# Routing steps of tokens 0 to 127: six per pair of gathers for pairs 0 to 16 and four for pairs 17 to 32, in place of six, five and four

## The reference, cut to what matters

```python
s = jnp.einsum('bshpd,hpkd->bshpk', q, sub_keys)
v_half, i_half = lax.top_k(s, PEER_TOPK)
cand = v_half[..., 0, :, None] + v_half[..., 1, None, :]
top_s, top_c = lax.top_k(cand.reshape(B, S, PEER_HEADS, PEER_TOPK * PEER_TOPK), PEER_TOPK)
experts = i1 * PEER_NKEYS + i2
g = jax.nn.softmax(top_s.astype(jnp.float32), axis=-1)
...
u = expert_u[ec]
act = jax.nn.gelu(jnp.einsum('cd,ced->ce', xc, u).astype(jnp.float32))
return jnp.einsum('ce,ced->cd', gc * act, expert_v[ec])
```

## Time and profile before

| | |
|---|---|
| median of 3 runs | 1257.31 us (1254.69 to 1258.04) |
| the profiled execution, its own time | 1260.68 us |
| its span | 1258.9 us |
| mean granted TensorE clock | 0.944 |
| busy: PE, DVE, ACT, POOL | 1078.0, 796.0, 456.8, 295.8 us |
| moved by DMA | 432.08 MB, mean 343 GB/s |

### The profile page before, as it was taken

One profiled execution on the slowest core, in us unless ns is written; L12 is line 12 of the kernel. 1 busy time (PEld: TensorE's weight loads), 2 busy tenths in 40 slices (PEclk: granted clock), 3 DMA queues, 4 the chain that ended last, 5 costly groups with the idle time before them and its releaser, 6 DMA issues.

```text
span 1258.9 us, 13841 instructions
## 1 busy us (share of the span) xinstructions
PE 1078.0 (86%) x5002; PEld 536.8 (43%) x5002; DVE 796.0 (63%) x1865; ACT 456.8 (36%) x1257; POOL 295.8 (23%) x261
## 2 busy tenths in 40 slices
PE   6998986977887676769988789968998998999998
PEld 2887572432343222313332344423443444565543
DVE  5567758887763999764457667576655477645201
ACT  1132127555342444443353343434334423332201
POOL 0000013434343344433323333332323000000000
PEclk9999987998898889989999899988999999999999
DMA  9987419999999999999999999999999975344573
GB/s 388 409 328 316 169 47 370 364 354 411 421 383 421 417 404 395 378 423 401 421 421 420 421 421 420 420 422 363 421 420 423 380 268 200 142 160 154 212 293 127
DMA packets 63487, 432.08 MB, mean 343 GB/s; under 512 B 6931, under 2 KB 10300, under 8 KB 11836
## 3 DMA queue, kind: packets, MB, share of 16 engines
q0 software_dynamic: 36864, 268.45, 52.4%
q1 hardware_dynamic: 26160, 161.76, 32.3%
q10 hardware_dynamic: 396, 0.99, 0.2%
HBM read 430.12 MB, written 1.06 MB: 343 GB/s over the span
## 4 chain that ended last, share of the span: by engine, by line
PE 51%; DVE 20%; DMA 19%; ACT 5%; issue 2%; POOL 1%; another core or an unknown queue 0%; SPq 0%; DVEq 0%
PE ps L1140 22%; DMA AR<-in_puv,idx 17%; PE ps L1095 10%; DVE AR L1722 7%; PE ps L771 4%; PE ps L1254 3%; PE ps L990 2%; DMA W<-in_w_mod 2%; PE ps L1121 1%; PE ps L806 1%; POOL AR L2513 1%; PE ps L1035 1%; ACT av L2258 1%; DVE RT L1694 1%; ACT acc L2137 1%
## 5 line engine op out<-in xcount | busy, mean ns | idle before, releaser
L2513 POOL DMA_INDIRECT AR<-in_puv,idx x256 | 295.5, 1154 | 675.4 <-PE ps L1095 433.1
L1095 PE MATMUL ps<-AR,acc 128*64 128x512 f32 x904 | 286.6, 672 | 100.2 <-ACT acc L2137 98.4
L1722 DVE CUSTOM_DVE_ANT_0 AR<-AR,mixT 128x1024 f32<-128x1024 f32 x128 | 153.5, 1222 | 69.6 <-DMA AR<-in_puv,idx 69.3
L1140 PE MATMUL ps<-W,AR 128*128 128x512 f32 x416 | 189.2, 598 | 0.7 <-ACT AR L2137 0.7
L1095 PEld LDWEIGHTS ps<-AR,acc 128*64 128x64 f32 x904 | 71.8, 146 | 263.8 <-ACT acc L2137 169.5
L1722 DVE CUSTOM_DVE_ANT_0 AR<-AR,tok 128x1024 f32<-128x1024 f32 x128 | 153.0, 1220 | 48.4 <-DMA AR<-in_puv,idx 48.3
L1140 PE MATMUL ps<-W,hT 128*128 128x512 f32 x320 | 158.4, 626 | 6.5 <-DVE PT L2029 5.2
L2256 ACT ACTIVATE av<-av 128x1 f32<-128x1 f32 x256 | 51.3, 200 | 286.7 <-DVE av L1722 286.1
L1140 PEld LDWEIGHTS ps<-W,AR 128*128 128x128 f32 x416 | 76.1, 191 | 78.8 <-issue 76.7
L1140 PEld LDWEIGHTS ps<-W,hT 128*128 128x128 f32 x320 | 58.1, 198 | 83.3 <-issue 74.7
L2137 ACT ACTIVATE acc<-fold,av 128x64 f32<-128x64 f32 x226 | 78.6, 348 | 7.4
(11 more groups left out here) (459 smaller groups left out, 1311.2 us busy)
## 6 DMA issues: line engine op xcount, KB each, us to landing
W<-in_w_in SPq DMA_DIRECT2D x90, 1024.0 KB, 11.5
W<-in_w_mod SPq DMA_DIRECT2D x24, 1024.0 KB, 16.0
W<-in_wba SPq DMA_DIRECT2D x8, 1024.0 KB
W<-in_wbb SPq DMA_DIRECT2D x8, 1024.0 KB
W<-in_wo SPq DMA_DIRECT2D x8, 1024.0 KB
W<-in_w_out SPq DMA_DIRECT2D x4, 1024.0 KB, 5.7
W<-in_wq SPq DMA_DIRECT2D x4, 1024.0 KB
AR<-in_puv,idx POOLq DMA_INDIRECT x256
```

The lines of the kernel that those rows point to most:

```text
L1095: t = mm(of(("E", a, c))[64 * g:64 * g + 64, :], dg_at((2 * p + g) % NDG, late), GB[:, places[g], D + c * 512:D + c * 512 + 512], start=(m ...
L1140: t = mm(b[:, :], src[:, k, :], slab(i)[:, k, :], start=(k == 0), stop=(k == 7))
L1722: ttr(GB[:, n, 0:D], GB[:, n, 0:D], H2[a][g], 1.0, 0.0, MUL, ADD, av[:, a, c:c + 1]).then_inc(*ve.sig("dot", p, g))
L2513: eng.indirect_dma_start(GB[:, n, :], None, puv, bass.IndirectOffsetOnAxis(ap=idx[:, a, c:c + 1], axis=0)).then_inc(*gp.dma(f"g{n}", "gat" ...
```

## The change

One line of `loop_chores`:

```diff
@@ -492,7 +492,7 @@
-        advance(routes, 6 if p < 8 else 5 if p < 16 else 4 if p < 33 else 8)
+        advance(routes, 6 if p < 17 else 4 if p < 33 else 8)
```

## The result

The changed kernel takes 1252.64 us (median of 13 runs, 1249.65 to 1256.56), the kernel before 1257.31 us on the same chip (13 runs). The ratio is 0.9969 with a 95% interval of 0.9957 to 0.998, 3.9 us less; on a second chip it was 0.996 (0.9945 to 0.9975), 5.0 us less. Forecast were 1250.5 us and 6.8 less.

The account below looks back on a forecast made before the run. Transferred bytes at about 421 GB/s were taken to bound the kernel from 183 to about 976 us, then PE. Terms of 2.0 and 4.8 us took 1257.3 to 1250.5 us; range 1246.5 to 1258, own range 1248.5 to 1253.

Parts of the forecast that it names:

- likeliest case: Both terms count: 1250.5 us, own range 1248.5 to 1253, chance 0.43.
- Hole 1: 268 to 281 us at 272 GB/s, 4.6 us missing; pair 16 was to be issued 4.0 us earlier, pair 17 2.0.
- The chain to the accumulation of pair 25: Pairs 15 to 25, through four attn_mm: its end was to come 2.0 us earlier.
- the hole at 348: 348 to 368 us at 359 GB/s, 2.9 us missing; said to be opened by lateness of pair 25's accumulation.
- term 1: Lead of the chain ending in pair 25's accumulation, 2.0 us; bounds 0 and 4.0.
- Term 2: 460 to 530 us: second routing one pair earlier removes most of DVE's lag, 4.8 us; bounds 0 and 6.2.
- hole 3: 460 to 530 us at 384 GB/s, 6.2 us missing; laid to DVE's lag from a 5.76 us wait for keys.
- Carried to the end undiminished: From pair 57 on the order stays nearly the old one, so the whole lead was to reach the end.
- Only term 2: Pairs 22 to 25 keep their time and the lead ends in a wider hole at 348: 1252.5 us, chance 0.13.
- Only term 1: 460 to 530 us comes with transposes and gates, not DVE's lateness: 1255.3 us, chance 0.16.
- GpSimd blocked by DVE: Denser DVE work ahead of pair 16 lengthens its issues, losing 1.0 us of term 1: 1251.5 us, chance 0.04.
- The rule by which HBM binds at about 358 GB/s: By it the stretches at 359 and 384 GB/s would be no holes and term 2 nothing.

Follow-up runs that it names:

- e_gexp: The changed kernel with gexp of heads 6 and 7 moved behind the weights of pair 27 instead of ahead of them; 1249.65 us, ratio to before 0.9931.
- e_keys: The kernel before, with only the matmul keys of the second routing moved ahead of the accumulation of pair 35 on PE; ratio to before 0.996.
- e_early: The changed kernel's steps up to pair 24, then three a pair to 32, so the second routing begins where before has it; 1254.82 us, ratio 0.9975.
- r_late: Repeat of e_late: before's steps up to pair 27, only the second routing begins one pair earlier; ratio to before 0.9976.
- e_seven: The changed kernel with seven steps instead of eight behind each pair of the second routing; ratio to before 0.9953, 5.9 us below before.
- early half: Only the first routing's steps moved earlier against the kernel before, timed as e_early and r_early; 3.2 us less as mean of 3.1 and 3.3.
- r_early: Repeat of e_early: first routing earlier, second routing beginning where before has it; 1255.23 us, ratio to before 0.9974.
- late half: Only the second routing begun one pair earlier against the kernel before, e_late and r_late taken together; 2.4 us less (1.2 to 3.6).
- r_after: The changed kernel itself, run again beside e_gexp on one chip; 1252.31 us, ratio to before 0.996.
- e_late: The kernel before's steps up to pair 27, six at pairs 28 to 32, then eight, so only the second routing begins one pair earlier; ratio 0.999.

## Why the prediction was nearly right

The sign, the two places and the order of the two terms in time were right; 6.8 us were forecast and 3.9 and 5.0 measured, with 1252.64 us inside the likeliest case's own range.

*Hole 1.* Pair 16 4.0 us earlier forecast, 4.1 measured; pair 17 2.0, measured 2.5; 340 GB/s or more, measured 352; a wait for `spread_g` of 1.0 us, measured 0.78. `take_i` ran at 268.34, which is 271.25 in before's times, against 271.6 forecast. It was no longer the last wait: the accumulation of pair 13 began at 267.51, and pair 16 was issued 2.2 us behind that, as long as I had given it to free the first buffer. (The printed releaser is a DVE row, as in before.)

*The chain to the accumulation of pair 25*, 2.0 us: from its rows at 346.82 in before and 341.81 in after it came 2.1 us earlier. On the way one sentence did not hold. `gexp` of heads 4 and 5 held back the weights of pair 17 by the 1.5 us forecast (the accumulation waits 4.22 us in place of 2.68), but "nothing waits for these" is wrong: pair 21, which takes the buffers of pair 17, was issued 1.0 us earlier than in before, where pair 19 still was 2.5. And I stopped at pair 25. The step that failed is the sentence that this chain's lateness opens the hole at 348, and that therefore its lead is term 1. The lead had two pairs more to go, through ACT, and I had followed `gexp` of heads 4 and 5 (ahead of the weights of pair 17) and not that of heads 6 and 7, which the same ten steps move into the slot ahead of the weights of pair 27. Its price was 2.84 us on ACT; in this profile the stretch missed 1.9 us more than in before, and with it out of that slot (e_gexp) the time was 2.7 to 3.7 us less.

*Term 2, 4.8 us.* The mechanism held: `keys` behind pair 34, the second dot of 36 at its landing, 0.8 us of hole 3 left for a forecast 1.35, so 5.4 us gained in the profile. Pair 40, though, came at 407.10, which is 410.0 in before's times and not "near 408", and the dots of 37 at 410.1 for 408.1. Alone term 2 was timed at 2.1 us, under half of the 4.8, alone in another way (e_keys) at 5.0. The size is open between these; the wait for `spread_g` that comes in some executions takes part of it.

*Carried to the end undiminished.* Nearly: counted from the first gather, pair 64's first dot led by 5.7 us, pair 72's issue by 4.5, the last gather's by 970.47 - 962.51 - 2.91 = 5.0. The slow slice late in the stream, where I had only feared a loss, went from 363 to 397 GB/s, and 560 to 700 us misses 2.0 us in place of 4.3; in e_early, r_late, e_keys and e_seven it misses 4.7 to 5.0, so this gain is not one that the change brings each time.

*Rivals.* "Only term 2" gave 1252.5 us, the time that came out, and for a related reason, a lead lost in the hole at 348. The early half alone is worth 3.2 us, so term 1 is not nothing by itself; but `gexp` stands elsewhere in that half, and within the whole change the 2.7 to 3.7 us that it costs can take all of this. That the forecast came near is thus in part luck: a cost that it left out met parts whose sizes are not known within 2 us. "Only term 1", at 1255.3, is what e_early and r_early measured (1254.82 and 1255.23), and their intervals do not part them from the whole change; against it speak the late half's own 2.4 us (1.2 to 3.6) and hole 3, closed in after and r_after and open in e_early and r_early. "GpSimd blocked by DVE" did not show at pair 16: its two issues took 0.94 and 1.32 us, and its full lead arrived. Of pair 17 the first took 1.80 us in place of 0.93, and that pair's lead was larger than forecast all the same. The rule by which HBM binds at about 358 GB/s (DMA: Bandwidth & Descriptors, Trainium skill, "Where 436 GB/s comes from") does not hold here: hole 3 went from 384 to 416 GB/s, 421 in e_seven, and time was gained.

## What to carry to other kernels

When steps are dealt out earlier, every step moves, also the ones that are far from the place you look at: list for each engine what now stands directly ahead of the instruction that frees a buffer, above all what switches ACT's function table. In these profiles a stall cost what the stream of transfers missed by it: the same 4.24 us wait cost bytes where the late gather was issued 1.5 us ahead of the last outstanding landing, and none where at least three gathers were still to land, the first of them 3.1 us behind the issue. And where one wait is the cause, move the one instruction that is waited for: three lines for `keys` were worth as much as ten steps moved, and three for `gexp` 2.7 to 3.7 us on top of these. Last, when the times of one kernel's executions part by some us on the way, give an experiment that must show 2 us its own neighbour on the same chip, as e_gexp has after.

## What the runs showed of the hardware

Two loads of ACT's function table with an exponential between took 2.84 us (1.28 each, 0.02 us ahead of the activation that follows). Executions of one kernel, with the same order on every engine, part ways within one or two pairs and keep the difference for six pairs or more: after and r_after by 2.2 us up to pair 24, e_late and r_late by 2.3 us up to pair 24 (kept to pair 27, 1.5 at pair 31), e_early and r_early by 2.3 us between pairs 28 and 29 (kept beyond pair 40). The profiles don't say which transfer decides it. The DMA engines moved 421 GB/s over the 70 us of e_seven's row above.
